# A hybrid decoder step on one core: reordered page, weight and branch transfers, tanh gates, and expert rows added by indirect transfers

## What is computed

```
p = x @ w_in                                   # branch inputs, and 3 x 1024 gate columns
o_fox(sample) = softmax attention over 2 gathered cache pages of 128 rows per sequence, and the new rows
br[j] = o[j] @ w_branch[j]                     # j = 0 (GLA), 1 (attention), 2 (short convolution), o[j] is 512 wide
mix = sum_j(sigmoid(gate[j]) * br[j]) @ w_out
x1  = LN(a * x + mix)                          # a = 2 ** 0.25
gate weights wt: best group of 4 experts, its top 2, renormalised
moe = sum over the 2 experts of wt * (silu(x1 @ w_gate[e]) * (x1 @ w_up[e])) @ w_down[e]
y   = LN(a * x1 + moe)
```

## Time and profile before

| | us |
|---|---|
| median of 3 runs | 1805.14 |
| lowest and highest | 1802.52, 1805.14 |
| the profiled execution, its own time | 1802.28 |
| its span in the trace | 1800.6 |
| stage_front and stage_fox | 0 to 760 |
| stage_gates | 760 to 1250 |
| stage_out | 1250 to 1387 |
| routing | 1392 to 1420 |
| expert tiles | 1420 to 1741 |
| tail | 1741 to 1800 |

### The profile page before, as it was taken

The page is one execution under the profiler, slowest core; times in us unless marked ns, Lnnn a source line. Parts: engine busy times, 40 slices in busy tenths (PEclk is TensorE's granted clock), DMA queues, the critical chain, the costliest instruction groups (busy, mean ns, idle before and its releaser), DMA issues. The chain is left out here.

```text
span 1800.6 us, 25640 instructions
## 1 busy us (share of the span) xinstructions
PE 1617.8 (90%) x9847; PEld 1480.2 (82%) x9847; DVE 839.0 (47%) x1335; ACT 657.6 (37%) x1088; POOL 230.1 (13%) x317
## 2 busy tenths in 40 slices
PE   7999999999989999988798999999997499999950
PEld 6988788889988888888798999999786388888830
DVE  3423453453033335512032321324543799999947
ACT  4422142212244444413111111112201388888852
POOL 1000120012001111120000000000000123333124
PEclk8999999999999999999899999999998599999975
DMA  6111231033212021151325113212321778988448
GB/s 173 39 36 37 72 110 48 26 95 123 88 34 78 28 68 49 40 191 25 129 59 170 36 36 135 71 36 82 91 75 55 245 272 277 349 295 299 166 142 249
DMA packets 155296, 208.27 MB, mean 116 GB/s; under 512 B 14835, under 2 KB 121347, under 8 KB 155176
## 3 DMA queue, kind: packets, MB, share of 16 engines
q1 hardware_dynamic: 132472, 130.86, 23.6%
q0 software_dynamic: 22704, 75.79, 12.5%
HBM read 161.78 MB, written 44.84 MB: 115 GB/s over the span
## 5 line engine op out<-in xcount | busy, mean ns | idle before, releaser
L382 PE MATMUL ps<-xh,slab_hi 128*128 128x384 f32 (+1 forms) x504 | 173.5, 344 | 1.8 <-DVE xl L741 1.8
L382 PE MATMUL ps<-xl,slab_hi 128*128 128x384 f32 (+1 forms) x504 | 166.8, 331 | 0.0
L382 PE MATMUL ps<-xh,slab_lo 128*128 128x384 f32 (+1 forms) x504 | 166.8, 331 | 0.0
L1876 PE MATMUL ps<-xh,slab_hi 128*128 128x384 f32 (+1 forms) x384 | 126.2, 329 | 4.8 <-DVE m L2075 4.1
L1876 PE MATMUL ps<-xl,slab_hi 128*128 128x384 f32 (+1 forms) x384 | 125.8, 328 | 0.0
L1876 PE MATMUL ps<-xh,slab_lo 128*128 128x384 f32 (+1 forms) x384 | 125.7, 327 | 0.0
L382 PEld LDWEIGHTS ps<-xh,slab_hi 128*128 128x128 f32 x504 | 96.4, 191 | 16.0 <-issue 12.0
L2072 DVE TENSOR_TENSOR gt_sg<-ps,gt_sg 128x384 f32<-128x384 f32 (+1 forms) x48 | 25.7, 534 | 163.9 <-PE ps L1876 163.9
L2747 PE MATMUL ps<-mo_hi_gu,mo_xh 128*128 128x512 f32 x256 | 101.1, 395 | 0.0
L2747 PE MATMUL ps<-mo_hi_gu,mo_xl 128*128 128x512 f32 x256 | 100.8, 394 | 0.0
L1876 PE MATMUL ps<-gt_oh,slab_hi 128*128 128x384 f32 (+1 forms) x288 | 95.0, 330 | 4.4 <-DMA gt_ol<-oT_lo 4.4
(11 more groups left out here) (470 smaller groups left out, 4263.3 us busy)
## 6 DMA issues: line engine op xcount, KB each, us to landing
slab_raw<-in_w_in SPq DMA_DIRECT2D x60, 512.0 KB, 4.1
mo_raw_g<-in_w_e_gate SPq DMA_DIRECT2D x16, 1024.0 KB, 6.5
mo_raw_u<-in_w_e_up SPq DMA_DIRECT2D x16, 1024.0 KB, 9.5
mo_raw_d<-in_w_e_down SPq DMA_DIRECT2D x16, 1024.0 KB, 5.1
y_dram<-mo_y POOLq DMA_DIRECT2D x32, 512.0 KB, 4.6
gt_oh<-oT_hi SPq DMA_DIRECT2D x3, 2176.0 KB, 8.3
gt_ol<-oT_lo SPq DMA_DIRECT2D x3, 2176.0 KB, 13.4
slab_raw<-in_w_branch SPq DMA_DIRECT2D x24, 256.0 KB, 5.3
```

What stands on the lines that cost most here:

```text
L382: mm = eng.matmul(out, w[:, b, k, :], x[:, k, t0:t0 + tn], start=(k == 0 and j == 0), stop=(k == KC - 1 and j == 2), skip_group_check=True)
L1876: last = eng.matmul(out, w[:, s % 2, c, wk, :], x[:, k, t0:t0 + tn], start=(k == 0 and i == 0), stop=(k == ks[-1] and i == 2))
```

## The change

Nine edits, in order of the program:

1. First branch gates: ACT writes tanh(x/2) in place of exp(-x) and of sigmoid. invert_gate goes. sigmoid(x) is (1 + tanh(x/2))/2: DVE's multiply adds 1 in the same instruction, and the factor 1/2 is put into branch 0's weights when they are split (gate_scale).
2. Each page's log-forget rows are loaded right after the page, with the same register; the wait for the attention stores goes (another place in SBUF). load_gates(2) comes after page 5 in place of page 9.
3. The value pages from number 4 on wait until 6 key pages are transposed, those from 10 on until 11 are.
4. load_gates(4) comes ahead of load_branch(0), behind the last score rows (s_mm 4). ACT runs first_gate(20) and (21) ahead of head_gates(4).
5. Set 4j+5 is loaded ahead of load_branch(j).
6. PE: the wait for all m_done at a branch's start goes, and each unit waits for its own PSUM bank. One gate unit of the second three is run ahead of the first three branch units.
7. The split of m for stage_out is done in two parts, chunks 0 to 2 first, the rest while PE works on those.
8. Each x1 tile is also written to a new tensor acc_dram. Both have 128 rows in front (a copy of tile 0's rows), and token rows are shifted by 128. Empty slots point to one of the 128 rows each (own).
9. POOL adds each expert tile to acc_dram with an indirect transfer that reads, adds and writes. Add i waits for add i-1 to have landed. The weights are divided by a, so that LN of x1 + moe/a with eps/a^2 is the same value. The tail becomes: wait for both y buffers, 9 plain loads of acc_dram by SP, sum and square sum on ACT, normalisation on DVE.

```diff
-                eng.activation(sh.m[:, fb, t0:t0 + tn], sh.ps[:, 0, 0:tn], ACT.Exp, scale=-1.0).then_inc(sh.sg_ready, 1)
+                eng.activation(sh.m[:, fb, t0:t0 + tn], sh.ps[:, 0, 0:tn], ACT.Tanh, scale=0.5).then_inc(sh.sg_ready, 1)
...
             for i in range(NP):
+                if i == 4:
+                    eng.wait_ge(k_tr, 6)
+                if i == 10:
+                    eng.wait_ge(k_tr, 11)
...
-            head_gates(sh, eng, 4)
-            for u in range(20, 24):
-                first_gate(u)
+            first_gate(20)
+            first_gate(21)
+            head_gates(sh, eng, 4)
+            first_gate(22)
+            first_gate(23)
...
             for j in (1, 2):
-                eng.wait_ge(m_done, UJ * j)
                 for s in range(4):
                     eng.wait_ge(split, 4 * j + 4 + s + 1)
-                    for c in range(2):
-                        gates(j, s, c)
-                        branch(j, s, c)
+                    gates(j, s, 0)
+                    gates(j, s, 1, [0])
+                    branch(j, s, 0)
+                    gates(j, s, 1, [1, 2])
+                    branch(j, s, 1)
...
-            def store(i):
+            def add_rows(i):
+                if i >= 1:
+                    eng.wait_ge(y_st[(i - 1) % RY], 16 * ((i - 1) // RY + 1))
                 eng.wait_ge(y_out, 2 * i + 2)
-                eng.dma_start(y_rows[i], y[:, i % RY, :]).then_inc(y_st[i % RY], 16)
+                eng.indirect_dma_start(out=sh.acc_dram[:, :],
+                                       out_offset=bass.IndirectOffsetOnAxis(ap=mo.slot_idx[:, i:i + 1], axis=0),
+                                       in_=y[:, i % RY, :], in_offset=None, compute_op=ALU.add).then_inc(y_st[i % RY], 16)
...
+            eng.wait_ge(tail_gu, 2 * NTILE + 2)
+            for i in range(RY):
+                eng.wait_ge(y_st[i], 16 * len(range(i, NTILE, RY)))
+            for t in range(NT):
+                t0 = tile_rows(t)[0]
+                eng.dma_start(total(t), sh.acc_dram[128 + t0:128 + t0 + 128, :]).then_inc(t_in[t], 16)
```

More of the change, by code:

```diff
@@ L1559, in gate_part, with gate_scale @@
     return slice(0, 8) if n < 4 else slice(8, 12) if n < 8 else slice(0, 12)
+def gate_scale(n):
+    return 0.5 if 4 <= n < 8 else 1.0
 def head_gates(sh, eng, n):
@@ L1721, in load_page, with load_logf @@
                               ).then_inc(k_in[i % RK], 16)
[L1723 to L1724 removed]
+                return n
+            def load_logf(i, n):
                 eng.dma_start(lf[:, i // NPAGE, i % NPAGE, :],
@@ L1753, in _ @@
             for j in (1, 2):
+                load_gates(sh, eng, 4 * j + 5)
                 eng.wait_ge(m_done, UJ * j)
                 load_branch(j)
-                for s in range(1, 5 if j == 1 else 4):
+                for s in range(2, 5 if j == 1 else 4):
                     load_gates(sh, eng, 4 * j + 4 + s)
@@ L1878, in units, with gates @@
                     last.then_inc(done, 1)
-            def gates(j, s, c):
-                units(j, s, c, "gate", lambda v: gate_bank(j, v), range(8), sh.xh, sh.xl, gate_mm)
+            def gates(j, s, c, groups=range(3)):
+                units(j, s, c, "gate", lambda v: gate_bank(j, v), range(8), sh.xh, sh.xl, gate_mm, groups)
             def branch(j, s, c):
@@ L1885, in branch @@
                     eng.wait_ge(o_in, 32 * j + 32)
-                units(j, s, c, "branch", branch_bank, range(4), oh, ol, br_mm)
+                units(j, s, c, "branch", branch_bank, range(4), oh, ol, br_mm, range(3))
             gate_pieces(24, FIRST)
@@ L2020, in _ @@
                         eng.activation(sh.slab_hi[:, 0:SLAB], sh.slab_raw[:, :], ACT.Copy).then_inc(sh.pre_head, 1)
+            eng.wait_ge(m_done, 3 * UJ - 12)
+            for t in range(3):
+                out_m_heads(sh, eng, t, slice(0, 3))
             eng.wait_ge(m_done, 3 * UJ - 2)
             for t in range(3):
-                out_m_heads(sh, eng, t)
+                out_m_heads(sh, eng, t, slice(3, KC))
         @block.vector
@@ L2128, in _ @@
                         accumulate(j, 6 * s + u)
+                        if j == 2 and s == 3 and u >= 3:
+                            out_m_tails(sh, eng, u - 3, slice(0, 3), 0)
                     if j == 1 or s < 2:
@@ L2135, in _, with stores_done @@
             for t in range(3):
-                out_m_tails(sh, eng, t)
+                out_m_tails(sh, eng, t, slice(3, KC))
 def tile_rows(t):
     return (128 * t, 0) if t < 8 else (TOK - 128, 64)
+def stores_done(n, i):
+    return 32 * n + (32 if i == 0 else 0)
 def stage_out(nc, sh):
@@ L2663, in _ @@
             note_d(NE - 1)
-            for t in range(NT):
-                if t % 4 == 0:
-                    if t < 8:
-                        gone = eng.value_load(mo.after[0:1, NE - 3 + t // 4:NE - 2 + t // 4], min_val=1, max_val=NTILE + 1)
-                        eng.wait_ge(tail_gu, 2 * gone)
-                    else:
-                        eng.wait_ge(tail_gu, 2 * NTILE + 2)
-                t0 = tile_rows(t)[0]
-                eng.dma_start(total(t), sh.x1_dram[t0:t0 + 128, :]).then_inc(x1_in[t], 16)
             for i, (dst, src) in enumerate(((gb, sh.ln2_g), (bb, sh.ln2_b))):
@@ L2703, in _ @@
                 if i >= RX + 3:
-                    store(i - RX - 3)
+                    add_rows(i - RX - 3)
             for i in range(NTILE - RX - 3, NTILE):
-                store(i)
-            for i in range(RY):
-                eng.wait_ge(y_st[i], 16 * len(range(i, NTILE, RY)))
-            def fetch(c, t, to, op=ALU.bypass):
-                eng.indirect_dma_start(out=to, out_offset=None, in_=sh.y_dram[:, :],
-                                       in_offset=bass.IndirectOffsetOnAxis(ap=sh.slots[:, c, t:t + 1], axis=0),
-                                       compute_op=op).then_inc(t_in[t], 16)
-            eng.wait_ge(tail_d, NTILE + 1)
-            eng.wait_ge(tail_gu, 2 * NTILE + 2)
-            eng.wait_ge(x_tr, 2 * NTILE)
-            for t in range(NT):
-                fetch(0, t, first(t))
-                if t < PLAIN:
-                    fetch(1, t, y[:, t, :])
-                else:
-                    eng.wait_ge(all_scaled, t + 1)
-                    fetch(1, t, total(t), ALU.add)
+                add_rows(i)
         @block.tensor
```

170 lines of the change are left out of this document (76 added, 94 removed).

## The result

| | us |
|---|---|
| before, median of 4 runs | 1805.14 |
| after, median of 4 runs (lowest, highest) | 1740.62 (1738.56, 1741.49) |
| ratio, 95% interval | 0.9641, 0.9624 to 0.9658 |
| predicted | 1749, range 1738 to 1778 |
| span of the profiled execution | 1739.1, clock 0.966 (before 1800.6, 0.953) |

The sign, the range and most of the mechanism held. Four of the terms were off in size, the loop of the expert tiles lost its time in another place than the one that was costed, and the chain of adds turned out to stand closer to its limit than the text said.

A forecast was written before the change was run, and what follows sets the result against it. TensorE, busy 90%, bounds the kernel with fixed work, so only its waits, slow clock and the tail can be won: 1802.3 - 41 - 2 - 13.8 + 2 = 1747.5, set to 1749 for the runs' median; range 1738 to 1778.

The forecast's parts named there:

- Gates and stage_out, -41: stage_gates and start of stage_out: PE's waits and slow clock go, 43.4 us, counted as 41; bounds 30 and 43.
- decay row: stage_gates: PE's 7.15 us wait for the decay row goes, with 2.0 us of slow clock behind it.
- key page: stage_gates: PE's 4.86 us wait for a key page goes with its slow clock, 8.0 us; lower bound nothing.
- branch weights: stage_gates: earlier gate weights remove PE's 9.12 us wait for a gate and its slow clock, 10.6 us.
- branches and stage_out: Branches 1 and 2, start of stage_out: waits for ol, m and m's split go with slow clocks, 15.6 us.
- Tanh, -2: stage_fox: reciprocals leave DVE, table loads leave ACT; PE's 2.4 us wait goes, counted 2, bounds 0 and 4.
- The tail, -13.8: After the last tile: last add 6 us, then plain loads, 3.2 us a tile on ACT; gains 13.8, bounds 8 and 16.
- The loop, +2: Expert tiles: adds land in 8 us, under the 9.35 us tile; added DMA traffic costs 2 us, bounds 0 and 15.
- (a): Expert tiles: adds late but not ruinous, landing 9.5 to 11 us; at 10.5 us, 26 us lost, 1775; chance 0.12.
- (c): Expert tiles: adds take over 11.5 us and bound the loop, slower than before; 1835 at 12.5 us; chance 0.06.
- (b): stage_gates: PE's waits come back since faster PE wants the same transfers earlier; gain 30, not 41, 1760; chance 0.12.
- (d): Tail bound by something else, such as serial loads or a table load per tile; gains nothing, 1762; chance 0.07.

The follow-up runs named there:

- the experiment: Changed kernel with tanh alone undone: exp, add and reciprocal in stage_fox, sigmoid in the first branch of stage_gates; 1745.70 us, ratio 0.9686.
- the last experiment: Changed kernel with ACT's square-root table loaded right after its last copy of y, and the last accumulator store of x1 on SP; 1738.86 us.
- The run with one transfer more: Changed kernel with one small 64-byte transfer, waited for, on POOL between an add's landing and the next add; 1804.61 us, ratio 1.0023.
- The run with two: Changed kernel with two small transfers, one after another, each waited for, on POOL between an add's landing and the next add; 1886.67 us, ratio 1.0477.

## Why the prediction was right, point by point

**What bounds the kernel.** It held: PE's work is unchanged, 50 of the 61 us came from stretches in which it waited or ran slow, 17 from the tail, and the loop and the borders gave 6 back. Between the two profiled executions the sum had -54.8 and measured is -61.5. The 6.7 us are 4.9 in the gates, 2.2 at tanh and 3.3 in the tail, less 1.8 in the loop and 1.9 at the border and in the routing.

**Gates and stage_out, -41 (worked out 43.4).** Measured -45.9, 2.9 above the bound of 43. The 2.4 us that I took off for thin margins were not needed: no margin failed. The other 2.5 are a wait of 0.7 that the list puts down to "issue" and that I left out, and 1.8 us that no list names. In this pair of traces the sizes of the waits and of the slow stretches were right. By experiment: decay row 12.0 to 12.2 (predicted 9.2), key page 5.2 by the totals and 2.8 by the pieces (8.0), branch weights 12.8 by the median and 11.1 without the stray slow stretch (10.6), branches and stage_out 8.4 + 4.2 and, inferred, 2.9 for edit 5, 15.5 in all (15.6). Each wait was read rightly to 0.6 us, except the key page's. What does not carry over from one execution to the next is the clock behind a wait: in the one that I read it was low for 3 to 6.7 us, behind the same waits in the experiments for 5 to 12.

**Tanh, -2.** Measured -4.2 between the traces, 3 to 4 by the means over the traces, at the bound of 4. The wait (2.4 in the earlier trace rows, 2.5 in the experiment) was right. The rest lies in the start, which scatters by 5 us with edit 1 in.

**Double stores of x1, 0.** The piece with x1 is 100.1 us in all traces: the cover held. The 0.5 us put with the loop was in fact 1.7 at the border, and not from the store's landing, as the last experiment shows. No run shows what it is from.

**The tail, -13.8.** Measured -17.1, above the bound of 16. Last add 5.9 (6), load 3.4 (4.3 by the earlier trace rows, a row from beside other traffic), ACT 2.87 a tile (3.2: I added 0.2 us of gaps to each tile that are not there, and used the passes of the earlier trace rows, 1.10, for one that takes 1.01), table load 1.28 (1.3), end 3.4 (3.4). The nine tiles make 3.0 us and the load 0.9; the last add started 0.7 us behind the last copy where I had 0.1, which takes 0.6 back: 3.3.

**The loop, +2.** Measured +3.8, inside 0 to 15, so the number came out near for another reason than the one given. I costed landing against tile, and ACT waited only 2.8 us for it. The step that failed is "Tile period 9.35 unchanged": it rose to 9.62 in the window, and by 0.12 us over the whole loop. What the traces show in its place is PEld's longer wait for L2889 (1.1 to 3.9 us), behind DVE's longer waits ahead of it (4.7 to 9.2). I had counted POOL's descriptor lists (2.45 us each) as free, since POOL has time. Whether it is they that make DVE wait stays open.

**The signs.** The three large gaps are gone, the clock is full, and the branch starts have no gap. The adds land in 8.3 us in the median, under the 9 of the text, but in 9.1 in the dense window, and ACT's wait for a transfer, which was the sign of trouble, has begun there.

**Rivals.** (a) and (c) were the right ones to fear. The run with one transfer more has a link of 11.54 us and ends level with before (0.2% above it), so the point from which the change would lose lies there, where the text had 11.5. The run with two is (c). (b) and (d) did not come.

## What to carry to other kernels

A wait of the matrix engine costs its length plus half of the slow stretch behind it, and that stretch can be longer than the wait; take it as a range, from several waits of the trace, and look at the order in which transfers are issued before anything else. A serial chain of transfers beside a loop is free only while its period, issue and landing together, is under the loop's: read the slack from how far the chain lags behind the producer's copy and from the producer's wait for the buffer, not from the queue's own wait, and test it with a small transfer put into the chain. When work moves to an engine that has time, look at the engine that feeds the fullest one, since it may wait longer although nothing of its own has changed.

## What the runs showed of the hardware that was not expected

- The stretch of half clock behind the same wait was 4.0 us in one execution (decay row) and 10.2 in another, behind 7.15 and 7.4 us of idle time.
- The clock also fell to 0.50 once with no gap: from about 842 to 852 us in the run with edit 4 undone, with PE busy in every microsecond. Ahead of it stood, in that trace, transposes and two groups of eight matmuls with 16 columns, between gate quarters. The same sequence ran at 1.00 in the trace of after.
- An indirect add of 128 rows of 4 KB into device memory took 5.9 us from its start to the next transfer with the queues idle, and 8.3 in the median over the loop (5.8 to 13.1); the same without the read 3.4 idle and 8.7 in the median. So the read costs 2.5 us with the queues idle, and under load none shows in these medians.
- A transfer of 64 bytes cost 3.5 us in the loop with its issue and wait, though transfers of 32 to 64 KB land after 1.8 to 2.1 us elsewhere in the trace of after.
